# A hybrid layer on one core: inputs laid out transposed with u projected k by k, and memory attention with probabilities divided before they are transposed

## The reference

```
proj = rms_norm(x) @ w_in                    # u (512), q, k, v (512 each)
y_ssm = s5_mixer(u, lam, log_step, b, c, d, w_glu, b_glu)
y_att = moba_attention(q, k, v, rel_bias)    # 8 heads of 64
h = x + concat(rms_norm(y_ssm), rms_norm(y_att)) @ w_out
# memory attention: 256 memory tokens, 4 heads of 128
q = rms_norm(rms_norm(h) @ x_wq);  k, v = rms_norm(mem) @ x_wkv;  k = rms_norm(k)
h = h + softmax(q k^T / sqrt(128)) v @ x_wo
h = h + conv_ffn(rms_norm(h))                # up to 2 x 2816, conv of 3 tokens, down
```

## Time and profile before

| what | value |
|---|---|
| median of 3 runs | 676.1 us (676.05 to 676.61) |
| the profiled execution | 676.84 us, its span 675.0 us |
| PE busy | 664.4 us, 98% |
| DVE busy | 489.7 us, 73% |
| ACT busy | 345.0 us, 51% |
| POOL busy | 178.6 us, 26% |
| DMA | 105.76 MB, mean 157 GB/s |
| granted TensorE clock | 1.00 throughout |

### The profile page before, as it was taken

How to read it: one execution, slowest core, us unless ns; L and a number is a source line. 1 busy time by engine, 2 the same in 40 slices (tenths; PEclk the granted TensorE clock), 3 DMA queues, 4 the chain that set the end, 5 groups by cost and what they waited for, 6 DMA issues and landing times.

```text
span 675.0 us, 10889 instructions
## 1 busy us (share of the span) xinstructions
PE 664.4 (98%) x4039; PEld 550.3 (82%) x4039; DVE 489.7 (73%) x807; ACT 345.0 (51%) x602; POOL 178.6 (26%) x184
## 2 busy tenths in 40 slices
PE   7999999999999999999999999999999999999997
PEld 6978877877778788888998888888888888888886
DVE  3999998849765657556877675666566687867967
ACT  4747654676844544664454433333333454554662
POOL 4899997033221101240101111011101121100000
PEclk9999999999999999999999999999999999999999
DMA  8737563577210215030337557555556446654563
GB/s 257 225 82 183 118 186 102 156 223 258 64 63 2 98 59 187 1 124 1 126 125 249 191 186 242 191 183 187 190 191 227 146 183 210 226 186 141 178 197 124
DMA packets 73919, 105.76 MB, mean 157 GB/s; under 512 B 21929, under 2 KB 48852, under 8 KB 72340
## 3 DMA queue, kind: packets, MB, share of 16 engines
q1 hardware_dynamic: 70612, 98.89, 45.3%
q10 hardware_dynamic: 3264, 6.31, 2.9%
HBM read 88.27 MB, written 17.31 MB: 156 GB/s over the span
## 4 chain that ended last, share of the span: by engine, by line
PE 82%; DMA 4%; POOL 4%; ACT 4%; SPq 3%; DVE 2%; issue 1%; DVEq 0%; ACTq 0%; POOLq 0%
PE pb L519 24%; PE pb L521 24%; PE pb L520 23%; PE pb L2000 7%; PE pb L2003 4%; POOL F L802 2%; ACT F L1022 2%; SPq L679 2%; DMA raw<-in_w_in 1%; DMA F<-F 1%; DMA raw<-in_x_wkv 1%; DVE F L1420 1%; DMA F<-scr_y 1%; SPq L692 0%; ACT xs L1022 0%
## 5 line engine op out<-in xcount | busy, mean ns | idle before, releaser
L519 PE MATMUL pb<-xs,wring 128*128 128x512 f32 (+1 forms) x448 | 165.3, 369 | 0.1
L521 PE MATMUL pb<-xs,wring 128*128 128x512 f32 (+1 forms) x448 | 164.2, 366 | 0.0
L520 PE MATMUL pb<-xs,wring 128*128 128x512 f32 (+1 forms) x448 | 164.1, 366 | 0.0
L1426 DVE SCALAR_TENSOR_TENSOR F<-pb,ccol,F 128x511 f32<-128x511 f32 x88 | 65.9, 749 | 71.7 <-ACT F L1022 69.9
L509 DVE TENSOR_TENSOR wring<-raw,wring 128x1024 fp32r<-128x1024 f32 x73 | 97.5, 1338 | 6.1 <-ACT wring L498 5.9
L519 PE MATMUL pb<-wring,xs 128*128 128x512 f32 x240 | 99.1, 413 | 0.5 <-DVE wring L512 0.3
L519 PEld LDWEIGHTS pb<-xs,wring 128*128 128x128 f32 x448 | 84.5, 189 | 14.5 <-issue 0.6
L521 PEld LDWEIGHTS pb<-xs,wring 128*128 128x128 f32 x448 | 84.5, 189 | 13.7
L520 PEld LDWEIGHTS pb<-xs,wring 128*128 128x128 f32 x448 | 84.5, 189 | 13.5
L521 PE MATMUL pb<-wring,xs 128*128 128x512 f32 x240 | 94.0, 392 | 0.0
L520 PE MATMUL pb<-wring,xs 128*128 128x512 f32 x240 | 93.7, 390 | 0.0
(11 more groups left out here) (160 smaller groups left out, 989.6 us busy)
## 6 DMA issues: line engine op xcount, KB each, us to landing
raw<-in_ffn_w_up SPq DMA_DIRECT2D x22, 1024.0 KB, 5.2
F<-in_ffn_w_down SPq DMA_DIRECT2D x11, 1024.0 KB, 5.0
scr_w<-F SPq DMA_DIRECT2D x11, 1024.0 KB, 3.9
F<-in_x SPq DMA_DIRECT2D x8, 512.0 KB, 5.9
raw<-in_w_in ACTq DMA_DIRECT2D x4, 1024.0 KB, 6.0
raw<-in_w_out SPq DMA_DIRECT2D x4, 1024.0 KB, 4.9
raw<-scr_w SPq DMA_DIRECT2D x8, 512.0 KB, 3.8
raw<-scr_w SPq DMA_DIRECT2D x15, 256.0 KB, 4.7
```

Source lines behind the costliest of these rows:

```text
L519: nc.tensor.matmul(ps, lh, rh, start=first, stop=False)
L520: nc.tensor.matmul(ps, lh, rl_, start=False, stop=False)
L521: return nc.tensor.matmul(ps, ll, rh, start=False, stop=last)
L1426: return V.scalar_tensor_tensor(out=o, in0=a, scalar=s1, in1=b, op0=o1, op1=o2)
```

## The change

Half one. The host hands x and mem over transposed too (`xt`, `memt`), and the small parameters as ready columns (`first`, `cols`, `ssm_b`, `ssm_c`). x and mem are still loaded in rows as well, for their squares. u is now made k by k: a piece is one or two of the eight 128-row slices of w_in's u columns with the same slices of x.T, and PE adds all four column blocks of u per slice, in four banks. ACT, DVE and PE split and use a piece as soon as it is there. All transposes of x, mem and parameters are gone from PE, and POOL's low part of unit 0. u leaves PSUM by ACT without the token factors; DVE multiplies these in afterwards in SBUF (u_scale). The token factors and the bias table follow q tiles on PE. SP waits for the x squares before it loads mem.

```diff
+PIECES = [(0, 1), (1, 1), (2, 2), (4, 2), (6, 2)]
...
+            for i in range(3):
+                piece_load(i)
+            sync.dma_start(bmat.rearrange("p i a c -> p (i a c)"), A["ssm_b"]).then_inc(b_in, 16)
+            x_load(0)
+            x_load(1)
+            piece_load(3)
+            piece_load(4)
+            x_load(2)
+            x_load(3)
...
+            sync.wait_ge(sq_done, TT)
             for t in range(MT):
                 sync.dma_start(memr[:, t, :], A["mem"][0, t * 128:(t + 1) * 128, :]).then_inc(mem_in, 16)
...
-            pool.wait_ge(hi_done, 1)
-            nc.gpsimd.tensor_tensor(w_unit(0, 1), raw_unit(0), w_unit(0, 0).bitcast(f32), ALU.subtract)\
-                .then_inc(lo_done, 1)
...
+            def piece_hi(i):
+
+                k, n = PIECES[i]
+                act.wait_ge(piece_in[i], 32)
+                ins = A_(piece_w(0, k, n), piece_raw(k, n), ACT.Copy)
+                ins.then_inc(hi_done if i else k0_hi, 1)
+                for d in range(k, k + n):
+                    ins = A_(xs[:, 0, d, :], xt[:, d, :], ACT.Copy, scale=nmix[:, d:d + 1])
+                ins.then_inc(u_hi, 1)
...
+            def piece_lo(i):
+
+                k, n = PIECES[i]
+                dve.wait_ge(hi_done if i else k0_hi, max(1, i))
+                ins = tt(piece_w(1, k, n), piece_raw(k, n), piece_w(0, k, n).bitcast(f32), ALU.subtract)
...
+                for d in range(k, k + n):
+                    ins = stt(xs[:, 1, d, :], xt[:, d, :], nmix[:, d:d + 1], xs[:, 0, d, :].bitcast(f32),
+                              ALU.mult, ALU.subtract)
+                ins.then_inc(u_lo, 1)
...
+            def u_scale(m):
+
+                if m == 0:
+                    after_drain(dve, "xb")
+                after_drain(dve, f"u{m}")
+                tt(uT[:, m, :], uT[:, m, :], xbc, ALU.mult).then_inc(u_ready, 1)
...
+            for i, (k0, n) in enumerate(PIECES):
+                if i == 0:
+                    pe.wait_ge(u_hi, 1)
+                    for m in range(4):
+                        fill(pe, f"u{m}")
+                        u_pass(m, 0, 0)
+                pe.wait_ge(u_lo, i + 1)
+                for k in range(k0, k0 + n):
+                    for m in range(4):
+                        for a in range(1 if k == 0 else 0, 3):
+                            last = u_pass(m, k, a)
...
             for t in range(TT):
                 proj_tile(13, U_V, "v", t)
-                m_transposes(t)
```

```diff
-        QXT_BANK, XO_BANK, W_BANK = (0, 1, 2, 0), (1, 0, 1, 7), (2, 1, 2, 0, 2, 1, 3, 2)
+        QXT_BANK, XPV_BANK, W_BANK = (0, 1, 2, 7), (7, 1, 7, 1), (2, 0, 2, 0, 2, 3, 0, 2)
...
+            def divide_by_sum(s):
+
+                after_drain(dve, f"xs{s}")
+                link(V.reciprocal(rl[:, s % 2:s % 2 + 1], lsum[:, 32 + s:33 + s]))
+                V.tensor_scalar_mul(pbuf[:, s % 2, 0:M], pbuf[:, s % 2, 0:M], rl[:, s % 2:s % 2 + 1])\
+                    .then_inc(xprob_ready, 1)
+
             row_max(0)
+            divide_by_sum(0)
             for s in range(TT * XH):
                 if s + 1 < TT * XH:
                     row_max(s + 1)
                 if s in (5, 9, 13):
-                    t = (s - 5) // 4
-                    normalise(f"xpv{t}", 32 + XH * t, XH, XD, t)
+                    xo_lo((s - 5) // 4)
...
+                if s + 1 < TT * XH:
+                    divide_by_sum(s + 1)
...
-                    last = mm(p[:, h * XD:(h + 1) * XD], ptb[:, s % 2, a * 128:(a + 1) * 128],
-                              xv[:, a, h * XD:(h + 1) * XD], a == 0, a == MT - 1)
+                    last = mm(p[:, h * XD:(h + 1) * XD], xv[:, a, h * XD:(h + 1) * XD],
+                              ptb[:, s % 2, a * 128:(a + 1) * 128], a == 0, a == MT - 1)
...
-                if s in (5, 9, 13):
-                    xo_transposes((s - 5) // 4)
```

More of the change, by code:

```diff
@@ L286, in plan @@
         def plan():
[L287 to L292 removed]
+            use(4, "xb"); use(6, "relb")
             for m in range(4):
@@ L1681, in _ @@
             dve.wait_ge(bias_in, 16)
-            def normalise(bank, l0, heads, width, t):
-                p = read(dve, bank)
-                link(V.reciprocal(rl[:, 0:heads], lsum[:, l0:l0 + heads]))
-                drained(tt(yrow[:, t, :].rearrange("p (h n) -> p h n", h=heads),
-                           p[:, :].rearrange("p (h n) -> p h n", h=heads),
-                           rl[:, 0:heads].unsqueeze(2).to_broadcast([128, heads, width]), ALU.mult), bank)
-                after_drain(dve, bank)
             def tile_lo(name, hi, lo, last=True):
@@ L1880, in _ @@
             xp_evac(dve, V.tensor_copy, TT * XH - 1)
-            normalise(f"xpv{TT - 1}", 32 + XH * (TT - 1), XH, XD, TT - 1)
             x3_rows(0)
+            xo_lo(TT - 1)
             w_residual(1, [1])
-            xo_lo(TT - 1)
             w_residual(2, [0])
@@ L2100, in _, with u_pass @@
-            for half in range(2):
-                for u in range(2):
-                    u_half(u, half)
-            def u_unit(m, halfway=None):
-                cols_unit(U_SSM + m, KD, lambda part, k: xs[:, part, k, :], [f"u{m}"], halfway)
+            for i in range(7):
+                mm(pb[7][:, 0:128], ident[:, :], ident[:, :])
+            def u_pass(m, k, n):
+                w = [piece_w(part, k, 1)[:, m * 128:(m + 1) * 128] for part in range(2)]
+                lh, rh = ((w[0], xs[:, 0, k, :]), (w[0], xs[:, 1, k, :]), (w[1], xs[:, 0, k, :]))[n]
+                return nc.tensor.matmul(pb[uses[f"u{m}"][0]][:, :], lh, rh, start=k == 0 and n == 0,
+                                        stop=k == KD - 1 and n == 2)
@@ L2571, in _, with columns, group_pairs, laid_out @@
             down_phase("d", NP, 3)
-INPUTS = ["x", "mem", "norm_mix", "w_in", "attn_qn", "attn_kn", "ssm_lam_re", "ssm_lam_im", "ssm_log_step",
-          "ssm_b_re", "ssm_b_im", "ssm_c_re", "ssm_c_im", "ssm_d", "ssm_w_glu", "ssm_b_glu", "gnorm_ssm",
-          "gnorm_attn", "w_out", "rel_bias", "norm_xattn", "norm_mem", "x_wq", "x_wkv", "x_wo", "x_qn",
-          "x_kn", "norm_ffn", "ffn_w_up", "ffn_conv_w", "ffn_conv_b", "ffn_w_down"]
+INPUTS = ["x", "mem", "w_in", "ssm_w_glu", "w_out", "rel_bias", "x_wq", "x_wkv", "x_wo", "norm_ffn", "ffn_w_up",
+          "ffn_w_down"]
+def columns(a):
+    return a.reshape(-1, 128).T
+def group_pairs(a, order):
+    return a.reshape((GP, 2) + a.shape[1:]).transpose(order).reshape(128, -1)
+def laid_out(inputs):
+    lam = [group_pairs(inputs[n][0], (1, 2, 0)) for n in ("ssm_lam_re", "ssm_lam_im")]
+    steps = np.repeat(inputs["ssm_log_step"][0].reshape(GP, 2).T, NS, axis=0)
+    gains = []
+    for name, k in GAINS:
+        g = inputs[name][0]
+        gains.append(columns(np.tile(g, 2) if name in ("attn_qn", "attn_kn") else g))
+    conv = [columns(inputs["ffn_conv_w"][0, i, 0]) for i in range(3)] + [columns(inputs["ffn_conv_b"][0])]
+    return {
+        "xt": inputs["x"][0].T,
+        "memt": inputs["mem"][0].T,
+        "first": np.concatenate([columns(inputs["norm_mix"][0])] + lam + [steps], axis=1),
+        "cols": np.concatenate(gains + conv, axis=1),
+        "ssm_b": np.concatenate([group_pairs(inputs[n][0], (1, 2, 0, 3)) for n in ("ssm_b_re", "ssm_b_im")], axis=1),
+        "ssm_c": np.concatenate([group_pairs(inputs[n][0], (1, 3, 0, 2)) for n in ("ssm_c_re", "ssm_c_im")], axis=1),
+    }
 def kernel(**inputs):
```

378 lines of the change are left out of this document (120 added, 258 removed).

## The result

The changed kernel takes 687.52 us (median of 4 runs, 685.25 to 689.76) against 676.08 (675.49 to 676.61): ratio 1.0168, 95% interval 1.0151 to 1.0185. It is 11.4 us **slower**; 672.9 was forecast. The profiled execution took 687.68, its span is 685.9.

A forecast was written before the change was run, and what follows sets the result against it. PE was taken to bound the memory attention, and a chain through DVE's power table and POOL's tables the start. 2.0 + 2.25 + 1.75 - 0.6 - 2.2 = 3.2 us gained, giving 672.9 us, range 669.3 to 675.4.

The forecast's parts named there:

- PE's own work: Start: u passes begin at 5.6 us, wait 2.1 for piece 2 and 3.9 for piece 3, end at 33.4.
- POOL cannot: Start: PE could reach kernels_in(0) at 47.7 us, but POOL's tables end only at about 52.2.
- DVE's turns keep their distance: Start: DVE's turns keep their distance with four u_scale (0.69 or more each) replacing the four u evacuations.
- The term 2.0: Start: outputs(1) begins at 86.6 us instead of 88.64, a gain of 2.0 with bounds 0 and 5.
- The fallen clock: Start: if PE is slow after its two waits, each costs 1.9 us, which its lead of 4.4 still covers.
- mem: Output of half one: mem's four transposes and a wait leave PE, a gain of 2.25 us, between 1.7 and 2.7.
- The xo transposes: Memory attention: four groups of xo transposes at 0.43 leave PE, a gain of 1.75 us.
- The divisions: Memory attention: 16 reciprocals and multiplies (0.3 each) on DVE are hidden except the first, costing 0.6 us.
- I count 1.1 for each, minus 2.2: Memory attention, heads 5 to 9: PE waits 1.1 us for POOL's low part and 1.1 for bank 7's gcol multiply.
- My bound of minus 4: Memory attention, heads 5 to 9: worst end for the minus 2.2 us, approached if divisions wait out POOL's low parts.
- The rival on the slower side: Memory attention: DVE and ACT set the head loop, exceeding 2.49 us per head; 678 us, chance 0.06.
- in kind, not in size: Memory attention: trace said to agree thus with the shared DVE and POOL port rule, under which divisions wait out 2.37 us.

The follow-up runs named there:

- e10: New start with DVE's last two turn steps moved early and u_scale reading token factors from PSUM, memory attention of the kernel before: 673.09 us.
- e3: The changed kernel with DVE's gcol multiply of the query tile ahead of xo_lo instead of behind it: 682.15 us.
- e9: e3 with ACT instead of DVE multiplying the probabilities by the reciprocal: 683.52 us.
- e1: The changed kernel with the memory attention of the kernel before, leaving the new start and the mem.T split: 677.81 us.
- e16: e13 with POOL computing only 16 columns of each of x_wo's four low parts: 676.55 us.
- e13: e3 with other banks for the last x_wo tiles, so the first up product does not take the last-but-one's bank: 680.25 us.

## Why the prediction was wrong

It went the other way than forecast, by 14.6 us. Point by point:

- **PE's own work**: right in kind, too hopeful in size. PE's busy time fell; its u passes begin at 7.5 (forecast 5.6: piece 0 was there at 6.2, not 4.5) and end at 36.1 (forecast 33.4). Of the two waits that I put into them only the second stands, 1.8 instead of 3.9. In place of the first, 2.1, the passes themselves were slow: the first 48 took 13.9 us instead of 10.9, the last 48 took 12.8.
- **"POOL cannot"**: half right. POOL's table moved as I said and further (50.1, forecast 52.2). The step that failed is the next one, "DVE's turns keep their distance". They stood behind u_scale in the program's order, as I had quoted it, and I priced u_scale by 0.69 "or more" without asking what two SBUF operands do beside POOL, although POOL was busy 24.70 of 25.48 us there and I had cited that rule for half two. The price stood in the trace of before (73.79, 1.52 each). I also missed that DVE's next low part waits for a high part behind PE's last u pass (6.05 idle), so that the turns wait for PE, whose lead I took to be free. The term 2.0 was -3.8 in this profile; e10 has it at +2.6 (outputs(1) at 86.03).
- **The fallen clock**: I held that the lead covers it. At the u passes it did in this execution (outputs(0) at 67.40, against 67.38 in e3, where the clock stayed up), but not where the fall lasted longer (68.64 in e9, 69.92 in e1). It did not at outputs(0) (1.2 us more for 96 passes) nor at head 10 (1.5).
- **mem**: 2.25 forecast, 2.6 measured.
- **The xo transposes**: their 1.75 is gone from PE, and little of it reached the end: in e16, with the long waits away, the memory attention takes 52.7 against 52.8. PE came earlier and then waited for DVE twice near the end, 0.86 and 1.06. That DVE, 10.85 of 12.10 us busy before the first up product, was the next bound there, I had not looked at.
- **The divisions**: the multiply is 0.35 (I took 0.3), the first one costs 0.4 (I took 0.6).
- **"I count 1.1 for each, minus 2.2"**: this term was -7.8: PE is 2.1 late at the first head's transposes (272.97 against 270.89) and 9.0 late at head 10, though two groups of xo transposes (0.9) are gone by then. I named the place and the bank rightly. But the wait for POOL's low part, to which I gave 1.1, was 0.3, and the wait behind bank 7, the other 1.1, was 3.0, because what I priced as two waits side by side is one chain: the division held by POOL (2.36), row maximum, exponential, xo_hi, xo_lo, gcol, each behind the other on an in-order queue, then the clock. My bound of minus 4 allowed for blocked divisions, not for the queue behind one. The wait of 3.0 alone is more than I gave for both. What fell is the step "I count 1.1 for each": e3, which takes only gcol out of that chain, gives 4.4 of the 7.8 back. (The stage adds up: -1.75 for the xo transposes, 0.4 for the first division, 7.8 here, 0.9 for a drain at 318.04 and 1.9 for the bank below make 9.25, against 9.2 read.)
- **The banks**: not in the sum at all. The new W_BANK puts a tile in the bank of the first up product (1.9, of which e13's trace gets 0.7 back).

The rival on the slower side had 0.06 and the wrong mechanism: no steady loop of heads exceeds 2.49 us (275.50, 277.99, 280.48 in the changed kernel), the loss is in single events. Its size, 678, was too small as well, also by its own sum: 8 less 1.75 is 6.25, not 5. Two rules would have raised it: the one on the shared port, which I set aside with "in kind, not in size", and the look at every new neighbour of a blocked operation.

What stays open: how e16's 3.7 us divide exactly between blocked operations and late low parts; and what decides whether the clock falls behind the wait for piece 3.
